# Outputs split inside four attentions, and output product, norm and query product of two cross attentions in one block

## The reference, cut to what matters

```python
# first block, twice: moba attention, then dsa attention
x = x + attention(rms_norm(x, ln_attn)) @ w_o
x = x + sq_relu_mlp(rms_norm(x, ln_mlp), w_up, w_down)
# second block, twice: rwkv7 + s5, then differential attention
h = h + y_mix                                   # y_mix ends in a product with hy_w_out or da_w_o
h = h + memory_cross_attention(rms_norm_2(h, norm_xattn), rms_norm_2(mem, norm_mem), ...)
h = h + swiglu(...)                             # second time moe_swiglu(...)

def memory_cross_attention(h, mem_n, w_q, w_kv, q_gain, k_gain, w_o):
    q = rms_norm_2((h @ w_q).reshape(b, t, MEM_HEADS, MEM_HEAD_DIM), q_gain)   # 4 heads of 256
    k, v = jnp.split(mem_n @ w_kv, 2, axis=-1)
    k = rms_norm_2(k.reshape(b, m, MEM_HEADS, MEM_HEAD_DIM), k_gain)
    p = jax.nn.softmax(jnp.einsum('bthd,bmhd->bhtm', q, k) * MEM_HEAD_DIM ** -0.5, axis=-1)
    return jnp.einsum('bhtm,bmhd->bthd', p, v).reshape(b, t, D_MODEL) @ w_o
```

## Time and profile before

| | us |
|---|---|
| median of three runs | 2759.71 |
| profiled execution, whole | 2757.09 |
| its span in the profile | 2755.0 |
| PE busy | 2527.3 |
| DVE busy | 1894.4 |
| ACT busy | 1510.0 |

### The profile page before, as it was taken

One profiled execution on the slowest core, in us unless ns is written; L12 is line 12 of the kernel. 1 busy time (PEld: TensorE's weight loads), 2 busy tenths in 40 slices (PEclk: granted clock), 3 DMA queues, 4 the chain that ended last, 5 costly groups with the idle time before them and its releaser, 6 DMA issues. The chain is left out here.

```text
span 2755.0 us, 37341 instructions
## 1 busy us (share of the span) xinstructions
PE 2527.3 (92%) x13506; PEld 2073.8 (75%) x13507; DVE 1894.4 (69%) x2295; ACT 1510.0 (55%) x1869; POOL 206.5 (7%) x224
## 2 busy tenths in 40 slices
PE   7899897997868799998979979999999999999998
PEld 6688775886766577887857758887887888888887
DVE  4566636666667565666556569896545989898898
ACT  4544435444320354544455458885444888888886
...
PEclk9999989999977899999989979999999999999999
...
GB/s 314 113 182 187 164 108 54 183 182 167 70 5 1 162 151 125 167 190 168 138 54 160 113 141 371 338 375 212 185 186 176 361 341 379 338 378 334 380 337 228
DMA packets 304904, 566.13 MB, mean 205 GB/s; under 512 B 21929, under 2 KB 126712, under 8 KB 304408
## 3 DMA queue, kind: packets, MB, share of 16 engines
...
...
## 5 line engine op out<-in xcount | busy, mean ns | idle before, releaser
L1684 DVE TENSOR_TENSOR weights_split<-ring,weights_split 128x1024 fp32r<-128x1024 f32 x676 | 814.8, 1223 | 214.4 <-ACT weights_split L1679 187.7
L1760 PE MATMUL ps<-weights_split,expert_split 128*128 128x512 f32 x3864 | 898.6, 392 | 5.5 <-DVE weights_split L1684 2.8
L1679 ACT ACTIVATE weights_split<-ring 128x1024 fp32r<-128x1024 f32 x676 | 715.2, 1061 | 306.5 <-PE ps L1760 295.4
L1760 PEld LDWEIGHTS ps<-weights_split,expert_split 128*128 128x128 f32 x3864 | 721.9, 188 | 157.2 <-DVE weights_split L1684 5.0
L287 DVE TENSOR_TENSOR weights_split<-ring,weights_split 128x2048 fp32r<-128x2048 f32 x182 | 420.1, 2309 | 335.4 <-ACT weights_split L278 331.7
L278 ACT ACTIVATE weights_split<-ring 128x2048 fp32r<-128x2048 f32 x182 | 344.8, 1895 | 314.2 <-PE ps L363 153.5
L457 PE MATMUL ps<-normed_split,weights_split 128*128 128x512 f32 x1248 | 448.5, 401 | 13.6 <-PEq L340 12.2
L458 PE MATMUL ps<-normed_split,weights_split 128*128 128x256 f32 x1248 | 353.3, 283 | 0.0
L363 PE MATMUL ps<-weights_split,source_split 128*128 128x512 f32 x1320 | 311.1, 392 | 20.0 <-DVE source_split L744 7.9
L363 PEld LDWEIGHTS ps<-weights_split,source_split 128*128 128x128 f32 x1320 | 245.4, 189 | 74.8 <-issue 14.6
L457 PEld LDWEIGHTS ps<-normed_split,weights_split 128*128 128x128 f32 x1248 | 239.2, 192 | 74.9 <-issue 17.1
...
## 6 DMA issues: line engine op xcount, KB each, us to landing
...
```

The costliest lines, as they stand in the source:

```text
L1679: nc.scalar.activation(split_piece(p, 0), ring_piece(p), ACT.Copy).then_inc(high.sem, 1)
L1684: nc.vector.tensor_tensor(split_piece(p, 1), ring_piece(p), split_piece(p, 0).bitcast(F32), ALU.subtract)\
L1760: last = nc.tensor.matmul(ps[:, banks[part if down else half][tt], :], stationary(s, k, tt), split_piece(p, i)[:, part * NW:(part + 1) * N ...
```

## The change

Three edits. First, `attention` gets a form `halved`, used by both causal `first_attention`s and both cross attentions: ACT's copy of an output goes into the high half of `normed_split` (`XS`), and DVE subtracts it from PSUM into the low half (`split_output`), four steps after the scores; PE waits for that split, not for the copy, before it uses the bank again. `project_mlp` and the last `project` then have no source to split. Second, the first part of `project_mlp` becomes a class `Joint`, and both cross attentions use it: their output product (of rwkv7/s5, and of the differential attention), the unscaled turned residual and the query product stand in one block with keys and values; `norm_stage` is gone there, and the memory's norm runs on ACT and DVE beside the first product tile, its load at the block's start. Third, as the query rows now lack the token's factor, the mean square of the residual times 256 EPS is put on a diagonal (`eps_row`) and two matmuls with ones add it to the queries' sums of squares. Unscaled turned rows are split into a buffer of their own (`rows_split`), and `XS` holds the source, later the MLP's hidden halves or the memory rows.

```diff
-    def __init__(self, core, name, gain_col, banks, scratch):
-        self.core, self.banks, self.scratch = core, banks, scratch
+    def __init__(self, core, names, gain_col, banks, scratch, rows, stat):
+        self.core, self.banks, self.scratch, self.rows, self.stat = core, banks, scratch, rows, stat
         which, r = gain_col
         self.gain = lambda k: core.cols[:, which, r + k:r + k + 1]
-        (self.added, self.turned, self.high, self.split, self.sums, self.sums_dve, self.inv) = (
-            core.sig(f"{name}_{n}") for n in ("rows", "turned", "high", "split", "sums", "sums_dve", "inv"))
+        self.added, self.turned, self.high, self.split, self.sums, self.sums_dve = (core.sig(n) for n in names)
...
-                last = core.nc.scalar.activation(core.XS[:, 0, k, :], self.place(k), ACT.Identity, scale=self.gain(k))
+                last = core.nc.scalar.activation(self.rows[:, 0, k, :], self.place(k), ACT.Identity, scale=self.gain(k))
...
+class Joint:
+    def __init__(self, core, flow, srcT=None, beside_act=None, beside_dve=None):
+        self.core, self.flow, self.srcT, self.beside_act, self.beside_dve = core, flow, srcT, beside_act, beside_dve
+        self.t0 = core.taken
+        core.taken += 4
+        self.src_hi, self.src_lo = core.sig("source_high"), core.sig("source_split")
+
+    def pe(self, e):
+        core, t0, xs = self.core, self.t0, halves(self.core.XS)
         for chunk in range(2):
             for j in range(2):
                 w = core.weights(e, t0 + 2 * chunk + j)
                 for tt in range(TT):
                     for k in range(4):
-                        if chunk == 0 and tt == 0 and k % 2 == 0:
-                            e.wait_ge(*src_lo.at(2 * j + k // 2 + 1))
-                        last = product(core, ps[:, 2 * chunk + tt, :], w, (ALL, k, ALL), xs,
+                        if self.srcT is not None and chunk + tt + k % 2 == 0:
...
+                    self.flow.pe(e, 0)
...
+    def act(self, e):
+        core, t0, pair = self.core, self.t0, self.pair
+        if self.srcT is not None:
+            for u in range(4):
+                core.nc.scalar.activation(pair(core.XS[:, 0], u), pair(self.srcT, u), ACT.Copy).then_inc(*self.src_hi.up())
         for i in range(4):
             core.hi(e, t0 + min(i + 1 + WS_BUFS, 5))
+            if i == 0 and self.beside_act:
+                self.beside_act(e)
             if i == 2:
-                flow.act(e, 0)
+                self.flow.act(e, 0)
         core.hi(e, t0 + 6)
-        flow.act(e, 1)
-        up.act(e)
-
-    def dve(e):
-        for u in range(4):
-            e.wait_ge(*src_hi.at(u + 1))
-            nc.vector.tensor_tensor(pair(source[:, 1], u), pair(srcT, u), pair(source[:, 0], u).bitcast(F32),
-                                    ALU.subtract).then_inc(*src_lo.up())
+        self.flow.act(e, 1)
...
+    def dve(self, e):
+        core, t0, pair = self.core, self.t0, self.pair
+        if self.srcT is not None:
+            for u in range(4):
+                e.wait_ge(*self.src_hi.at(u + 1))
+                core.nc.vector.tensor_tensor(pair(core.XS[:, 1], u), pair(self.srcT, u),
+                                             pair(core.XS[:, 0], u).bitcast(F32), ALU.subtract).then_inc(*self.src_lo.up())
...
         for i in range(4):
             core.lo(e, t0 + min(i + 1 + WS_BUFS, 5))
+            if i == 0 and self.beside_dve:
+                self.beside_dve(e)
             if i == 1:
                 add(0)
                 add(1)
             if i == 2:
-                flow.dve(e, 0)
+                self.flow.dve(e, 0)
         add(2)
         add(3)
-        flow.dve(e, 1)
+        self.flow.dve(e, 1)
         core.lo(e, t0 + 6)
-        flow.squares_dve(e)
+        self.flow.squares_dve(e)
...
+def project_mlp(core, gain_col, n, gated=False, beside=None, sp=None):
+
+
+
+
+    guard = core.scoped("rows_split", [P, 2, KD, T], F32R)
+    flow = Turn(core, NORM_SIGNALS, gain_col, (4, 5, 6, 7), [core.a(10240, D), core.a(11264, D)], guard.__enter__(),
+                core.stat)
+    joint = Joint(core, flow)
...
+    out_split = core.sig("source_split") if halved else kept
+    flat = lambda v: v.rearrange("p a t -> p (a t)")
...
-                    e.wait_ge(*kept.at(t - 1))
+                    e.wait_ge(*out_split.at(t - 1))
...
-                nc.scalar.activation(oT[:, t * nd:(t + 1) * nd, :].rearrange("p a t -> p (a t)"),
-                                     core.ps[:, 6 + t % 2, 0:nd * T], ACT.Copy).then_inc(*kept.up())
+                to = core.XS[:, 0] if halved else oT
+                nc.scalar.activation(flat(to[:, t * nd:(t + 1) * nd, :]), core.ps[:, 6 + t % 2, 0:nd * T], ACT.Copy)\
+                    .then_inc(*kept.up())
+
+    def split_output(e, t):
+        hi, lo = (flat(core.XS[:, i, t * nd:(t + 1) * nd, :]) for i in range(2))
+        e.wait_ge(*kept.at(t + 1))
+        nc.vector.tensor_tensor(lo, core.ps[:, 6 + t % 2, 0:nd * T], hi.bitcast(F32), ALU.subtract).then_inc(*out_split.up())
 
     def dve(e):
-        for s in range(steps + 1):
+        for s in range(steps + (4 if halved else 1)):
...
+            if halved and s >= 4:
+                split_output(e, s - 4)
...
-    norm_stage(core, core.x, core.XS, at_col("norm_xattn_2", 8 * layer), 0, extra_sp=sp)
...
-    with core.scoped("memory_split", [P, 2, KD, T], F32R) as MS:
-        qkv_normed(core, 1, gain, qk, vN, (mem, MS, mem_gain, mem_landed))
+    with core.scoped("rows_split", [P, 2, KD, T], F32R) as rows:
+        flow = Turn(core, FLOW_SIGNALS, at_col("norm_xattn_2", 8 * layer), (4, 5, 6, 7), [a(11264, D), a(10240, D)], rows,
+                    core.row_stat)
+        qkv_normed(core, 1, gain, qk, vN, (mem, core.XS, mem_gain, mem_landed), joint=(flow, srcT), sp=sp)
...
+    def mem_act(e):
+        e.wait_ge(*mem_landed.at(16))
+        nc.scalar.activation(core.a(4096, D), mem[:, 0, :], ACT.Square, accum_out=st[:, 0:1]).then_inc(*mem_sums.up())
+        for tt in range(TT):
+            e.wait_ge(*(mem_sums, mem_sums_dve)[tt].at(1))
+            nc.scalar.activation(st[:, 2 + tt:3 + tt], st[:, tt:tt + 1], ACT.Sqrt, scale=1.0 / D,
+                                 bias=eps(E_EPS, P)).then_inc(*mem_root.up())
+
+    def mem_dve(e):
+        e.wait_ge(*mem_landed.at(16))
+        V.tensor_tensor_reduce(out=core.a(5120, D), in0=mem[:, 1, :], in1=mem[:, 1, :], scale=1.0, scalar=0.0,
+                               op0=ALU.mult, op1=ALU.add, accum_out=st[:, 1:2]).then_inc(*mem_sums_dve.up())
+        for tt in range(TT):
+            e.wait_ge(*mem_root.at(tt + 1))
+            V.reciprocal(st[:, 4 + tt:5 + tt], st[:, 2 + tt:3 + tt]).then_inc(*mem_inv.up())
+            e.wait_ge(*mem_inv.at(tt + 1))
+            V.tensor_scalar(mem[:, tt, :], mem[:, tt, :], st[:, 4 + tt:5 + tt], None, ALU.mult).then_inc(*mem_scaled.up())
+
+    before = Joint(core, flow, joint[1], mem_act, mem_dve) if joint else None
+    q_rows = flow.rows if joint else core.XS
+    unit0 = 4 if joint else 0
...
+            if u == 3 and joint:
+                e.wait_ge(*eps_made.at(1))
+                for tt in range(TT):
+                    nc.tensor.matmul(ps[0:R, SUMS, tt * P:(tt + 1) * P], c("ones")[:, 0:R],
+                                     eps_row[:, tt * P:(tt + 1) * P], start=False, stop=False)
...
+        if joint:
+            before.pe(e)
...
+            if u == 0 and joint:
+                for b in range(4):
+                    if b == 1:
+                        flow.pe(e, 1)
+                    e.wait_ge(*flow.split.at(b + 1))
+                    for t in range(2):
+                        for k in (2 * b, 2 * b + 1):
+                            last = one_product(t, k)
...
+        if joint:
+            before.act(e)
+            flow.squares_act(e)
...
-                nc.scalar.activation(root, ps[0:R, SUMS, 0:T], ACT.Sqrt, bias=eps(E_EPS256 if one else E_EPS64, R))\
+                nc.scalar.activation(root, ps[0:R, SUMS, 0:T], ACT.Sqrt, bias=0.0 if joint else eps(E_EPS64, R))\
...
+        if joint:
+            before.dve(e)
+            flow.mean(e)
             for tt in range(TT):
-                e.wait_ge(*mem_root.at(tt + 1))
-                V.reciprocal(st[:, 4 + tt:5 + tt], st[:, 2 + tt:3 + tt]).then_inc(*mem_inv.up())
-                e.wait_ge(*mem_inv.at(tt + 1))
-                V.tensor_scalar(mem[:, tt, :], mem[:, tt, :], st[:, 4 + tt:5 + tt], None, ALU.mult).then_inc(*mem_scaled.up())
+                last = V.tensor_scalar(eps_row[:, tt * P:(tt + 1) * P], c("ident"), flow.stat[:, 2 + tt:3 + tt], 256 * EPS,
+                                       ALU.mult, ALU.mult)
+            last.then_inc(*eps_made.up())
...
-    project(core, YT)
...
-        e.wait_ge(*sig("source_split").at(4))
...
-    cross_attention(core, w, 0, at_col, 8192)
-    project_mlp(core, view(OT, 8), at_col("norm_ffn_2"), FF2 // NF, gated=True)
+    cross_attention(core, w, 0, at_col, 8192, view(0, 8))
```

(6 more changed lines are left out.)

114 lines of the change are left out of this document (52 added, 62 removed).

## The result

| kernel | median us (lowest to highest) | ratio to the kernel before, 95% interval |
|---|---|---|
| before, beside it | 2757.86 (2756.57 to 2760.87) | 1 |
| changed | 2743.2 (2732.27 to 2749.74) | 0.9940 (0.9922 to 0.9958) |
| changed, later (`e1_same`) | 2738.42 (2735.84 to 2741.12) | 0.9931 (0.9915 to 0.9948) |
| changed, later (`e9_changed`) | 2741.64 (2729.59 to 2745.73) | 0.9940 (0.9927 to 0.9953) |

The change is faster, by 0.6 to 0.7%: 0.006 x 2758 = 16.5 us to 0.0069 x 2758 = 19.0 us. The sum had promised 24.9.

The account below looks back on a forecast made before the run. PE, busy 92% of the span, was taken as the bound. Joins 20.6 plus heads and bodies 4.3 gave 24.9 us off 2757.09, so 2732.2; the profiled run being 2.6 under the median, 2734.8 us, range 2729.0 to 2743.0.

Parts of the forecast that it names:

- The sum: Whole kernel: joined blocks' 20.6 us plus 4.3 us net from attention heads and bodies, a gain of 24.9 us.
- Joined blocks: Both cross attentions, first output product to end of first query tile: gains 11.77 and 10.37 us, 20.6 after added work.
- (a) Side work: Joined blocks: the memory's norm beside the first products delays a weight split, costing 0.35 us a block.
- the rival's mechanism: Joined blocks: memory norm and rows' mean hold PE through DVE's strict order; 5 us a block, 2744.8 us, chance 0.12.
- Heads: Start of what follows each attention: 1.38 us gained per causal, 1.1 per cross attention; 5.6 with the last `project`'s 0.64.
- the first tile's own waits: First product tile after each attention: waits for later source pieces disappear, 5.82 - 5.44 = 0.38 us.
- The last `project`: Final output projection: its tiles lose their waits for source splits, 4 x 0.16 = 0.64 us.
- the rival on the clock: Shorter idle keeps PE's clock up at both joined blocks and last `project`: 4.6 us more gain, 2730.2 us, chance 0.06.
- Bodies: Causal attentions' steps: DVE's added output splits cost 0.3 us in the first, 1.0 in the second; cross attentions nothing.
- the slower rival: Attention steps: DVE's split waits for ACT's copy, so engines run one after the other; 9.6 us slower, 2769.3, chance 0.03.
- these 0.16 us are the waits ahead of every second k: Later product tiles, 5.60 us in `project` against 5.44 in the MLP: difference laid to source waits, which the change removes.
- the gain should stand at these places alone: Sign to check: only joined blocks and what follows attentions get faster; the mixture of experts keeps its length.

Follow-up runs that it names:

- `e1_same`: Changed kernel, unaltered, run again later; 2738.42 us, 0.9931 of the kernel before.
- `e9_changed`: Changed kernel, unaltered, run again beside `e10_back` on the same chip; 2741.64 us, 0.9940 of the kernel before.
- `e10_back`: Changed kernel without row_stat's 16 added bytes and with the buffers of before at three of four joined places; 2735.66 us, 0.9925 of the kernel before.
- `e4_joins`: Kernel before plus only the joined blocks of both cross attentions and the 16 bytes of row_stat, attention outputs written whole; 2739.92 us, 0.9938 of the kernel before.
- `e12_double`: Kernel of `e10_back` with the memory's two sums of squares done twice in each joined block, results unused; 2738.25 us, 0.9925 of the kernel before.
- `e6_swap`: Kernel before with only the exchange of buffers in the three MLPs, nothing moved or added; 2763.20 us, 1.0012 of the kernel before.
- `e2_unused`: Kernel before plus 16 unused bytes allocated behind stat, shifting every buffer allocated later; 2759.97 us, 1.0015 of the kernel before.
- `e8_pad64`: Kernel before plus 64 unused bytes allocated behind stat; 2766.95 us, 1.0028 of the kernel before.

## Why the forecast was right in most of its mechanisms, and 6 to 8 us off

**Joined blocks: right.** Forecast 31.25 and 31.40 us for the stretches; 31.71 and 32.09 in the changed kernel, 31.35 and 31.74 in `e10_back`, whose project tiles take the 5.44 us that the forecast had assumed. The low clock stayed at the first tile (0.95 and 0.94 over the blocks), and the query tile ran at 1.00 in `e10_back`. PE was idle for under 1 us. Gain 11.31 + 9.68 = 21.0 us in the first profile, and 21.2 (`e4_joins`) by the times, against 20.6.

**(a) Side work: right, at the edge.** 0.35 us a block had been taken. PE's idle time of 0.23 us in `e10_back`'s blocks is that of the MLP's head before (0.24), so the trace shows none of the 0.35. `e12_double` shows that the rival's mechanism was real and began 1 us further on.

**Heads: the waits right, the first tile's term wrong.** Each causal head was to give 1.38 us and gave 2.21 - 1.23 = 0.98; each cross head 1.1 and gave 2.43 - 1.71 = 0.72. The wait until PE starts (1.0 and 0.74) was right. The 0.38 for "the first tile's own waits" was not there: in `e10_back`, without any such wait, the first tile of the last `project` still takes 1548.69 - 1542.91 = 5.78 us and the next one 5.44, and the first MLP, counted from its first product, takes 209.88 us, in the kernel before 209.65. So a first tile is longer for another reason, which stays open. That makes 3.4 us instead of 4.96. The split out of PSUM took 0.42 and 0.69 us, the 0.417 and 0.682 taken. The Trainium skill (Perfetto Trace Analysis, Optimizing Scalar/DVE Operations) states a larger overhead for DVE on PSUM than on SBUF; the trace does not agree, with 0.69 us out of PSUM against the 0.686 of the earlier trace rows out of SBUF.

**The last `project`: near in size, wrong in reason.** 0.64 us had been expected from waits that go, with the 0.38 of its first tile 1.0; 1.55 came. The tiles stayed at 5.60 us without any wait; what went is the slow first tile, 24.19 us at 0.93 to 22.64 us at 1.00. That is part of the rival on the clock (1.8 us). Heads and `project` gave 3.4 + 1.55 and the bodies took 0.87, which is 4.1 us for the 4.3 of the forecast: the size is right because misses cancel, and that is luck.

**The clock at these starts: a gain that one profile could not show.** Each kernel has four such starts, at the three MLPs and the last `project`. `e6_swap` has this at its first MLP, whose first product is at 128.88:

```profile
136.36 1.92 ACT L278 ACTIVATE weights_split<-ring 128x2048 fp32r<-128x2048 f32 x1 [4.98 <-PE ps L363]
```

Its first tile took 136.36 - 128.88 = 7.48 us, where the kernel before took 5.82. In the five profiles of kernels with whole outputs (before, `e2_unused`, `e8_pad64`, `e6_swap`, `e4_joins`), where PE is idle for 2.26 to 2.47 us ahead of the start, 12 of the 20 first tiles took 7.3 to 7.5 us and 8 took 5.8 to 6.0. In the nine profiles of kernels with halved outputs, where PE is idle for 1.27 to 1.75 us, all 36 took 5.8 to 6.0. So the halved attentions keep the clock up at all four starts, not at one. By an estimate from this count that is worth 4 x 12/20 x 1.5 = 3.6 us in a mean execution; the profile of before happened to have one slow start, and the forecast read the other three as safe.

**Bodies: right.** 0.3 and 1.0 us; 0 and 0.87. In the loop DVE's splits had no idle time before them, so the slower rival did not come.

**The step that failed** is the sentence "these 0.16 us are the waits ahead of every second k", with the silence on the MLPs that followed from it ("the gain should stand at these places alone"). The row was read rightly, 5.60 us against 5.44 in the earlier trace rows, but the two tiles differ in two things: the waits and the buffer, `normed_split` against `source_split`. The same rows hold both names. Had the buffer been seen as the cause, the diff would have told that it moves under every product with tokens in the MLPs. Measured: 11.21 for 11.00 us a pair, 3.7 us in the first MLP, 1.5 in the second. The third is no longer as a whole, but 24 of its tiles at full clock took 135.10 us for 134.19. `e6_swap` gives 3.3 us by the times. That the forecast's error stayed at 6 to 8 us is partly luck, since gains that nobody had foreseen stand against this loss, as the table shows.

The whole span can be cut at the borders used above. Change against before in us, by the sum, in the three profiles of the changed kernel (first, `e1_same`, `e9_changed`) and in `e10_back`:

| stretch, length before | sum | changed | `e10_back` |
|---|---|---|---|
| start to first MLP, 127.90 | -0.7 | +0.2, -1.0, -0.9 | -2.0 |
| first MLP, 209.65 | -0.4 | +3.7, +3.6, +3.8 | +0.2 |
| to second MLP, 115.44 | 0 | -1.3, -0.5, -2.2 | -2.3 |
| second MLP, 219.69 | -0.4 | +1.5, +1.4, +1.2 | +1.5 |
| mixers, 271.00 | 0 | +5.8, -0.5, -6.7 | +5.7 |
| first block, 43.02 | -11.4 | -11.3, -10.8, -10.2 | -11.7 |
| rest of cross attention, 90.72 | -0.3 | +0.4, +0.6, +0.6 | 0.0 |
| third MLP, 222.42 | -0.4 | 0.0, -1.4, -1.3 | -1.5 |
| to second block, 131.63 | 0 | +0.3, -2.7, -0.7 | -1.0 |
| second block, 41.77 | -10.0 | -9.7, -9.0, -9.7 | -10.0 |
| rest of cross attention, 90.71 | -0.3 | +0.4, +0.6, +0.6 | 0.0 |
| last `project`, 24.19 | -1.0 | -1.6, -1.6, -1.6 | -2.2 |
| to the end, 1166.86 | 0 | +1.1, +1.7, 0.0 | +1.7 |
| span | -24.9 | -10.4, -19.6, -27.2 | -21.5 |

The three profiles average -19.1 us, where the times say 16.5 to 19.0. Against the sum they miss 5.3 us in the three MLPs (1.1 of it the first tiles' 0.38 each), 1.8 in the two rests (0.5 each of it is gone in `e10_back`, where the memory stands in another buffer; 0.35 each stays open) and 1.2 in the blocks; 2.4 us came unforeseen in the two stretches ahead of the second MLP and of the second block, for no reason that a run isolated. The mixers swing by 12.5 us between profiles of one program. The forecast's range had no such swing in it: the times of before had shown 2.7 us of spread, and later sets of the same kernel lay between 2749.25 and 2766.61.
